# The expert sub-layer's second table: half of its columns by dense products of the whole table, the other half gathered

## The chip, the cores and the metric

The kernel runs on one core of a Trainium2 chip. The metric is device microseconds of one execution, the median of three runs. Engines are named as the profile names them: PE (TensorE matmul), PEld (TensorE weight load), DVE (VectorE), ACT (ScalarE), POOL (GpSimd), SP (SyncE, which here issues DMA alone).

## The reference

One decoder block over 256 tokens of width 2048: a token-mixing sub-layer (two attention mixers that share one input projection), then a channel-mixing sub-layer, PEER. The change is in the second. For each token and each of 8 heads, a product-key search picks 16 of 128 x 128 experts; an expert is one row of `u` and one of `v`, both 16384 x 2048 in float32 (128 MiB each):

```
s1, i1 = lax.top_k(s[:, :, :, 0], PEER_TOPK)          # 16 of 128 first keys
s2, i2 = lax.top_k(s[:, :, :, 1], PEER_TOPK)          # 16 of 128 second keys
expert = i1 * 128 + i2 of the best 16 of 16 x 16 sums;  gate = softmax(top_s)
act = gelu(einsum('cd,ced->ce', hs, u[es]))           # 128 dots of 2048 for each token
y   = einsum('ce,ced->cd', gs * act, v[es])           # weighted sum of 128 rows of v
```

So a token needs 128 rows of `u` and 128 of `v`, 8 KB each. The result is normalised, gated and added to the token.

## The kernel before, in words

Everything is float32. Tokens lie on the 128 partitions, in two tiles (t = 0, 1). Engines run their own instruction streams and meet at semaphores; the order of each stream is written out by hand. The first 700 us (projections, the first tile's attention and mixing) are not touched. From there on:

*First tile's experts beside the second tile's attention and projections.* All engines walk 132 slots `s` (`SLOTS`). In slot `s` DVE takes the dot of the first tile's expert `s` (`dot0`, L2261: multiply a gathered row of `u` by `h2[0]`, both in SBUF, and sum), then a piece of the second tile's attention (slots 5 to 60: `mask_max`, `normalise`, with ACT's exponential between them) or of its projections (`second_projections`, slots 61 to 119: branch outputs, output projection, norms, expert queries), and in some slots a quarter of the next head's top-k (`topk_parts`, L2146). ACT turns four dots into gelu, DVE multiplies by the gates (`coefs`), ACT spreads each coefficient over a diagonal (`diags`, L1003), and PE adds four 512-column products of that diagonal and a gathered row of `v` (`v_row0`, L1644) into four PSUM banks. 192 weight tiles of 512 KB come by SP's queue, the second tile's 96 in a ring of four.

*Gathers.* POOL fetches one row for each of 128 tokens by an indirect DMA (`fetch`, L642, 1 MB): one `u` and one `v` row for each slot, in rings of five; then, for the second tile, in rings of eight, in batches of four (`batch`, L678). An index row is copied to `idx_now` for each head (`take`).

*Second tile's experts.* Eight heads (`unit` on each engine, six of them in a loop): DVE's dots (L2291) and the next head's top-k, ACT's gelu and diagonals, PE's products (L1708) into the other four banks. The first tile's end (`finish(0)`) lies inside the first head, the second's (`finish(1)`) is the kernel's end.

Of the kernel before, what the change touches and what calls it, by code (L numbers as in the profile page):

```python
# [6 lines left out]
ALU = mybir.AluOpType  # L7
# [36 lines left out]
RING0 = 5  # L44
BATCH = 4

# [11 lines left out]
class Chain:  # L58


    def __init__(self, eng, sem):
        self.eng, self.sem, self.n, self.i, self.step = eng, sem, 0, None, 0
# [6 lines left out]
    def wait(self):  # L69
        self.eng.wait_ge(self.sem, self.n if self.i is None else self.i * self.step + self.n)  # L70
# [4 lines left out]

    def enter(self, i, step):
        self.i, self.step, self.n0 = i, step, self.n

    def leave(self, times):
        assert self.n - self.n0 == self.step, (self.n - self.n0, self.step)  # L80
        self.n, self.i = self.n0 + times * self.step, None


def build(nc, x, c, positions, ada_w, ada_b, attn_pre_g, attn_post_g, w_in, cmp_pe, cmp_w1, cmp_b1, cmp_w2,
# [16 lines left out]
    with ExitStack() as ctx:  # L101
# [10 lines left out]
        o_w = o_a + AR * KW  # L112
        o_p = o_w + WR * KW
        o_g = o_p + PR * KW
        o_e = o_g + GR * KW
        o_f = o_e + ER * KW
        o_c = o_f + FR * KW
        o_i = o_c + ACCR * KW
        o_s = o_i + IR * KW
# [88 lines left out]
        gate_f_row = at(o_f + 8 * KW, D)  # L208
# [4 lines left out]
        diag = [at(o_e + 16 * KW + P * i, P) for i in range(8)]  # L213
        sq_junk = at(o_s, NC)
        early_u = [o_f, o_c, o_e, o_e + 8 * KW, o_a]
        early_v = [o_w + 8 * KW, o_w + 16 * KW, o_w + 24 * KW, o_w, o_a + 8 * KW]
        Urow0 = [at(o, D) for o in early_u]
        Vrow0 = [at(o, D) for o in early_v]
        first_free = (PH * TOPK) % RING0
        slots_u = [o_p, o_p + 8 * KW, o_p + 16 * KW] + early_u[first_free:] + early_u[:first_free]  # L220
        slots_v = [o_f + 16 * KW, o_f + 24 * KW, o_i] + early_v[first_free:] + early_v[:first_free]
        Urow = [at(o, D) for o in slots_u]
        slot_sem = [5, 6, 7] + [(first_free + i) % RING0 for i in range(RING0)]
        sem_base = [16 * len(range(i, PH * TOPK, RING0)) if i < RING0 else 0 for i in slot_sem]
        Vrow = [at(o, D) for o in slots_v]
# [31 lines left out]
        mtmp = mod_rows_sb  # L257
# [126 lines left out]
        OUTS = GROUPS + PAIRS  # L384


        LAG = 4
        SLOTS = PH * TOPK + LAG
        FIRST1 = 5
        MIX1 = FIRST1 + 2 * UNITS + 8  # L390
# [142 lines left out]
        def _(pool):  # L533
# [113 lines left out]
            def u_row0(i):  # L647
                u, e = i // TOPK, i % TOPK
                if e == 0:
                    take(u, u % 2)  # L650
# [1695 lines left out]
```

## Time and profile before

| | |
|---|---|
| median of three runs | 2146.29 us (2141.3 to 2150.93) |
| profiled execution: span, first to last instruction | 2140.2 us |
| busy: PE, PEld, DVE, ACT, POOL | 1912.1, 879.8, 1176.6, 389.3, 790.7 us |
| DMA | 821.41 MB, mean 384 GB/s |
| of it, gathers and POOL's other loads (q0) | 637.58 MB, 72.6% of 16 engines' span |
| chain that ended last | PE 51%, DMA 36%, POOL 5%, issue 4%, DVE 3% |

The profile is of one execution. A group of instructions is told by its line in the kernel, its engine and operation, what it writes and reads, and its count; then the time in which at least one of them ran, the mean duration of one, and how long the engine stood idle just before them with what ended the idleness. Busy time of PE overlaps itself, since its matmuls are pipelined. The DMA share is the time that packets took over 16 engines' time, and can come out a little above 1.

### The profile page before, as it was taken

Reading aid. Unit: us, or ns where it says so; the run is one execution under the profiler, and the core shown is the slowest. Engines: PE = TensorE matmul, PEld = TensorE weight load, DVE = VectorE, ACT = ScalarE, POOL = GpSimd, SP = SyncE. Lnnn points to the kernel's source line nnn. Section 1 sums busy time; section 2 is a strip of 40 time slices with the busy share of each in tenths; the row PEclk is TensorE's granted clock in tenths of the full one; section 3 lists DMA queues with packets and bytes.
Section 4 is the critical chain, followed back from the end, with each engine's and each line's share of the span. In section 5 each row is a group of like instructions: output and inputs, shape, how many; then the busy total and the mean of one; then the engine's idle time right before and its main releaser. Section 6 shows DMA issues by size and latency. Waiting matters only on the chain.

```text
span 2140.2 us, 15920 instructions
## 1 busy us (share of the span) xinstructions
PE 1912.1 (89%) x5111; PEld 879.8 (41%) x5111; DVE 1176.6 (55%) x2072; ACT 389.3 (18%) x994; POOL 790.7 (37%) x711
## 2 busy tenths in 40 slices
PE   5999999999999889999999989997778678688687
PEld 3444454444444344554443334442233233233233
DVE  5788657624113567778344445345655655655644
ACT  3111021122211143444010111110201101101101
POOL 4322131100000345666222334456354464454453
PEclk9999999999999999999999999999888889889888
DMA  9999969976897999999999999999999999999997
GB/s 343 367 378 397 374 230 378 373 250 217 284 344 247 386 399 413 417 421 419 417 417 418 417 418 419 417 419 422 422 421 422 422 422 419 422 422 422 422 422 315
DMA packets 161616, 821.41 MB, mean 384 GB/s; under 512 B 17136, under 2 KB 23632, under 8 KB 86796
## 3 DMA queue, kind: packets, MB, share of 16 engines
q0 software_dynamic: 92160, 637.58, 72.6%
q1 hardware_dynamic: 67492, 182.12, 23.5%
q10 hardware_dynamic: 1896, 0.86, 0.2%
q8 instruction: 36, 0.59, 0.1%
q14 instruction: 32, 0.26, 0.0%
HBM read 818.37 MB, written 2.13 MB: 383 GB/s over the span
## 4 chain that ended last, share of the span: by engine, by line
PE 51%; DMA 36%; POOL 5%; issue 4%; DVE 3%; ACT 0%; DVEq 0%; POOLq 0%; SPq 0%; ACTq 0%
PE PS L1153 15%; PE PS L1648 12%; DMA arena<-in_peer_u_dram,idx_now 11%; DMA arena<-in_peer_v_dram,idx_now 11%; PE PS L1609 10%; POOL arena L643 5%; PE PS L1708 5%; DMA arena<-in_peer_w_q_dram 4%; DMA arena<-in_ada_w_dram 4%; DMA arena<-in_w_out_dram 3%; DMA arena<-in_w_branch_mla_dram 2%; PE PS L1215 2%; DVE arena L1779 1%; PE PS L1359 1%; PE PS L1577 1%
## 5 line engine op out<-in xcount | busy, mean ns | idle before, releaser
L1708 PE MATMUL PS<-arena 128*128 128x512 f32 x1008 | 487.1, 647 | 141.0 <-DMA arena<-in_peer_v_dram,idx_now 140.7
L643 POOL DMA_INDIRECT arena<-in_peer_v_dram,idx_now x256 | 356.3, 1392 | 581.9 <-PE PS L1648 323.0
L1648 PE MATMUL PS<-arena 128*128 128x512 f32 x1024 | 471.9, 605 | 20.8 <-DMA arena<-in_peer_v_dram,idx_now 20.8
L2291 DVE CUSTOM_DVE_ANT_0 arena<-arena 128x2048 f32<-128x2048 f32 x128 | 291.9, 2292 | 253.9 <-DMA arena<-in_peer_u_dram,idx_now 253.6
L2264 DVE CUSTOM_DVE_ANT_0 arena<-arena 128x2048 f32<-128x2048 f32 x128 | 292.7, 2290 | 199.0 <-DMA arena<-in_peer_u_dram,idx_now 196.5
L1708 PEld LDWEIGHTS PS<-arena 128*128 128x128 f32 x1008 | 207.6, 209 | 420.4 <-issue 387.6
L643 POOL DMA_INDIRECT arena<-in_peer_u_dram,idx_now x256 | 320.0, 1250 | 147.9 <-issue 70.7
L1609 PE MATMUL PS<-arena 128*128 128x512 f32 x688 | 316.3, 601 | 19.0 <-DMA arena<-in_peer_w_q_dram 9.4
L1153 PE MATMUL PS<-arena 128*128 128x512 f32 x720 | 321.0, 596 | 1.4 <-ACT arena L765 1.4
L1648 PEld LDWEIGHTS PS<-arena 128*128 128x128 f32 x1024 | 191.6, 193 | 253.3 <-issue 220.5
L1609 PEld LDWEIGHTS PS<-arena 128*128 128x128 f32 x688 | 126.3, 190 | 192.4 <-issue 140.8
L1153 PEld LDWEIGHTS PS<-arena 128*128 128x128 f32 x720 | 133.8, 191 | 150.6 <-issue 145.2
L1824 DVE SCALAR_TENSOR_TENSOR arena<-arena,csil 128x2048 f32<-128x2048 f32 x60 | 141.0, 2350 | 19.7 <-DMA arena<-in_ada_w_dram 18.4
L556 POOL DMA_DIRECT2D arena<-in_ada_w_dram x64 | 33.9, 529 | 291.7 <-DVE arena L1824 210.0
L1215 PE MATMUL PS<-arena 128*128 128x512 f32 (+1 forms) x320 | 132.9, 573 | 4.5 <-DVE arena L1759 4.4
L1779 DVE SCALAR_TENSOR_TENSOR arena<-arena,csil 128x512 f32<-128x512 f32 x120 | 90.2, 751 | 20.3 <-DMA arena<-in_ada_w_dram 16.1
L1123 ACT ACTIVATE act_g<-dots 128x4 f32<-128x4 f32 x32 | 6.6, 205 | 500.5 <-DVE dots L2291 500.5
L1005 ACT ACTIVATE arena<-ident,coef 128x128 f32<-128x128 f32 x254 | 81.1, 389 | 82.6 <-DVE coef L2259 82.6
L1215 PEld LDWEIGHTS PS<-arena 128*128 128x128 f32 x320 | 60.6, 193 | 70.7 <-issue 65.0
L544 POOL DMA_DIRECT2D arena<-in_ada_w_dram x64 | 48.0, 754 | 87.5 <-DVE arena L1779 80.7
L638 POOL COPY idx_now<-idx_next 128x16 uint32<-128x16 uint32 x16 | 5.5, 341 | 194.5 <-DVE idx_next L2173 194.4
L1988 DVE CUSTOM_DVE_ANT_0 arena<-PS,causal 128x128 f32<-128x128 f32 (+1 forms) x96 | 30.4, 354 | 66.6 <-PE PS L1359 41.2
(290 smaller groups left out, 1177.0 us busy)
## 6 DMA issues: line engine op xcount, KB each, us to landing
arena<-in_ada_w_dram POOLq DMA_DIRECT2D x64, 1024.0 KB, 8.0
arena<-in_w_in_dram SPq DMA_DIRECT2D x112, 512.0 KB, 8.2
arena<-in_ada_w_dram POOLq DMA_DIRECT2D x64, 512.0 KB, 12.5
arena<-in_w_out_dram SPq DMA_DIRECT2D x64, 512.0 KB, 10.2
arena<-in_peer_w_q_dram SPq DMA_DIRECT2D x64, 512.0 KB, 10.9
arena<-in_w_branch_nsa_dram SPq DMA_DIRECT2D x32, 512.0 KB, 10.0
arena<-in_w_branch_mla_dram SPq DMA_DIRECT2D x32, 512.0 KB, 10.5
arena<-in_x_dram SPq DMA_DIRECT2D x4, 1024.0 KB, 7.8
```

The source lines that it names most:

```text
L544: pool.dma_start(place[:, :, seg, :], ada_v[:, j:j + rows_, c0:c0 + s * P]).then_inc(ada_in[n % ADA_SLOTS], 16)
L643: pool.indirect_dma_start(dst, None, tab, bass.IndirectOffsetOnAxis(ap=idx_now[:, now, e:e + 1], axis=0)).then_inc(landed, 16)
L1005: nc.scalar.activation(diag[e % 8], ident[:, :], ACT.Copy, scale=coef[:, e:e + 1]).then_inc(diag_ready, 1)
L1153: ins = nc.tensor.matmul(PS[:, bank + t, 0:cols], lhs[:, kk, t * P:(t + 1) * P], wring[:, m % WSLOTS, k, 0:cols], start=(kk == 0), stop=(k ...
L1215: ins = nc.tensor.matmul(PS[:, bank + t, 0:cols], hT[:, kk, t * P:(t + 1) * P], wring[:, m % WSLOTS, i, 0:cols], start=(kk == k1), stop=(k ...
L1609: ins = nc.tensor.matmul(PS[:, 4 + a % 2 * 2 + b, :], lhs[:, k, :], tile[:, b * NC:(b + 1) * NC], start=first, stop=last)
L1648: ins = nc.tensor.matmul(PS[:, k, :], diag[i % 8], Vrow0[i % RING0][:, k * NC:(k + 1) * NC], start=(i == 0), stop=False, skip_group_check= ...
L1708: ins = nc.tensor.matmul(PS[:, 4 + k, :], diag[e % 8], Vrow[e % RING][:, k * NC:(k + 1) * NC], start=(first and e == 0), stop=False, skip_ ...
L1779: ins = v.scalar_tensor_tensor(out=part, in0=w, scalar=csil[:, j:j + 1], in1=part, op0=ALU.mult, op1=ALU.add)
L1824: ins = v.scalar_tensor_tensor(out=acc, in0=w, scalar=csil[:, j:j + 1], in1=acc, op0=ALU.mult, op1=ALU.add)
L2264: v.tensor_tensor_reduce(row, row, h2[0], 1.0, 0.0, ALU.mult, ALU.add, dots[:, i % TOPK:i % TOPK + 1]).then_inc(u0_free, 1)
L2291: v.tensor_tensor_reduce(row, row, h2[1], 1.0, 0.0, ALU.mult, ALU.add, dots[:, e:e + 1]).then_inc(u_free, 1)
```

## The change

The 2048 columns of `v` are split at `CD = 1024`.

*Columns 1024 to 2047* are still gathered, as half rows of 512 KB for 128 tokens. The first 64 half rows of the first tile (`V0_ROWS`) are fetched between the second tile's `u` rows and summed on PE with diagonals; the other 192 are fetched behind the last `u` row, in a ring of four (`VRING`), and added on DVE into PSUM (`v_added`).

*Columns 0 to 1023* are computed as a dense product. For each tile a matrix A of 128 x 128 x 128 (first key, second key, token) is built on chip, 64 KB on each partition: the coefficients and both key numbers are turned with PE so that the 128 picks lie on partitions; for each token DVE makes a one-hot of the second key times the coefficient and a one-hot of the first key (`hots`, four tokens at a time, ACT does part of the scaling in `hot_times`), PE multiplies them (`a_rows`), ACT keeps the result (`a_kept`). Then the whole left half of `v` is read in 128 blocks of 128 rows x 1024 columns (512 KB, by SP's queue, a ring of six), and PE multiplies each with both tiles' slices of A. The second tile's A is built while the first 24 blocks (`NB`) go by for the first tile alone; these 24 are read again at the end for the second tile: 152 block reads.

Around it: no row of `v` is fetched in the slots of the first tile (128 slots instead of 132); the rings of `u` rows have eight places throughout; 22 of the first tile's dots and 15 of the second's are multiplied on POOL and summed on ACT (`POOL_ROWS`); from the 17th on, dots read `h2` from PSUM, to which ACT copies it; gelus and coefficients lag by one batch of four; both tiles are finished at the kernel's end; the loops over heads are unrolled; buffers move.

```diff
-RING0 = 5
 BATCH = 4
+CD = 1024
+VRING, DRING = 4, 6
...
+        ROWS = PH * TOPK
+        POOL_ROWS = tuple(range(20, ROWS, 5)) + tuple(range(ROWS + 4, 2 * ROWS - 8, 8))
+        V0_ROWS = ROWS // 2
+        NB = 24
+        BLOCKS = [(j, (0,)) for j in range(NB)] + [(j, (0, 1)) for j in range(NB, NK)] + [(j, (1,)) for j in range(NB)]
...
@@ sync: _(sp) @@
+            sp.wait_ge(u_free, dve_rows(2 * ROWS - 24))
+            sp.wait_ge(u_summed, pool_rows(ROWS))
+            for n, (j, tiles) in enumerate(BLOCKS):
+                if n < 2:
+                    sp.wait_ge(v_free, V0_ROWS)
+                elif n < DRING:
+                    sp.wait_ge(u_free, dve_rows(2 * ROWS))
+                    sp.wait_ge(u_summed, pool_rows(2 * ROWS))
+                else:
+                    sp.wait_ge(d_used, n - DRING + 1)
+                sp.dma_start(Vblk[n % DRING], v_tab[j * P:(j + 1) * P, 0:CD]).then_inc(w_landed[n % DRING], 16)
+                if n == 64:
+                    mod_row(gate_f_row, 3, row_in[0])
...
@@ gpsimd: _(pool) @@
+            def u_product(i):
+                pool.wait_ge(u_in[i % RING], 16 * (i // RING + 1))
+                pool.wait_ge(h2_ready[i // ROWS], 1)
+                row = Urow[i % RING]
+                pool.tensor_tensor(row, row, h2[i // ROWS], ALU.mult).then_inc(u_times, 1)
...
+                if n >= VRING:
+                    pool.wait_ge(v_free, n - VRING + 1)
+                fetch(v_halves, Vrow0[n % VRING], idx_v[0][:, n:n + 1], v_in[n % VRING])
...
+            for i in range(2 * ROWS):
+                u_row(i)
+                if i - RING + 1 in POOL_ROWS:
+                    u_product(i - RING + 1)
+                if i >= ROWS + RING and i % 2 == 0:
+                    v0_row((i - ROWS - RING) // 2)
+            for n in range((ROWS - RING) // 2, V0_ROWS):
+                v0_row(n)
+            for n in range(2 * ROWS - V0_ROWS):
+                v_row(n)
...
@@ scalar: _(act) @@
+            def row_summed(i):
+                act.wait_ge(u_times, pool_rows(i + 1))
+                row, e = Urow[i % RING], i % TOPK
+                nc.scalar.activation(row, row, ACT.Copy, accum_out=dots[:, e:e + 1]).then_inc(u_summed, 1)
...
@@ tensor: _(pe) @@
+            def a_rows(m):
+                t = m // 32
+                pe.wait_ge(hot_scaled, m + 1)
+                if m % 32 >= 2:
+                    pe.wait_ge(a_out, m - 1)
+                for k in range(4):
+                    ins = nc.tensor.matmul(PS[:, 4 * t + m % 2, k * P:(k + 1) * P], hot2[t][m % 2][:, k, :],
+                                           hot1[m % 2][:, k, :], start=True, stop=True)
+                ins.then_inc(a_in, 1)
...
+            def block_products(n):
+                j, tiles = BLOCKS[n]
+                pe.wait_ge(w_landed[n % DRING], block_landed(n))
+                for t in tiles:
+                    for k in range(2):
+                        ins = nc.tensor.matmul(PS[:, 4 * t + k, :], A_T[t][:, j, :], Vblk[n % DRING][:, k * NC:(k + 1) * NC],
...
+            turn_stats(1)
+            pe.wait_ge(a_out, 32)
+            n = 0
+            for m in range(32, 64):
+                a_rows(m)
+                if (m - 31) * NB // 32 > n:
+                    block_products(n)
+                    n += 1
+            pe.wait_ge(a_out, 64)
+            for n in range(NB, len(BLOCKS)):
+                block_products(n)
...
@@ vector: _(dve) @@
+            def hots(m):
+                t, tok = m // 32, 4 * (m % 32)
+                if m >= 2:
+                    dve.wait_ge(a_in, m - 1)
...
+            def v_added(n):
+                t, k = (0, V0_ROWS + n) if n < ROWS - V0_ROWS else (1, n - (ROWS - V0_ROWS))
+                dve.wait_ge(v_in[n % VRING], 16 * ((V0_ROWS + n) // VRING + 1))
+                sums_t = PS[:, 4 * t + 2:4 * t + 4, :].rearrange("p a b -> p (a b)")
+                dve.wait_ge(v_free, V0_ROWS + n)
...
+            for m in range(32, 64):
+                hots(m)
+                if m % 2:
+                    v_added(n)
+                    n += 1
+            for n in range(n, 2 * ROWS - V0_ROWS):
+                v_added(n)
+            finish_first()
+            finish_second()
```

## Rows read from the trace of the kernel before

**Rows 1.** the stretches; columns: us, busy (count) by engine, PE clock, DMA share, GB/s
```profile
...
735.00:1021.00 286.00, 276.65 (x944) 139.24 (x943) 203.12 (x465) 111.72 (x283) 170.60 (x120) 0.98 1.01 414
1021.00:1480.00 459.00, 432.29 (x1029) 184.74 (x1027) 210.65 (x325) 63.26 (x146) 179.71 (x139) 0.99 1.02 418
1480.00:2123.00 643.00, 501.48 (x1035) 213.50 (x1036) 363.14 (x552) 73.59 (x203) 319.00 (x258) 0.87 1.01 422
...
```

**Rows 2.** PE's groups, 1021 to 1480 us: busy us, mean ns, idle before
```profile
...
L1609 PE MATMUL PS<-arena 128*128 128x512 f32 x384 | 183.3, 606 | 12.3 <-DMA arena<-in_w_out_dram 6.1 <-DMA arena<-in_peer_w_q_dram 2.7 <-DMA arena<-in_w_branch_mla_dram 1.9
...
L1525 PE MATMUL PS<-arena,mod_rows_sb 128*128 128x128 f32 x32 | 4.2, 275 | 0.0
...
```

**Rows 3.** DMA queues from 703 us (packets, MB, share); issues (KB, us to landing)
```profile
...
q0 software_dynamic: 73728, 536.90, 89.9%
q1 hardware_dynamic: 15997, 58.15, 10.2%
...
arena<-in_w_out_dram SPq DMA_DIRECT2D x32, 512.0 KB, 12.6
...
```

**Rows 4.** VectorE's groups, 735 to 1021 us
```profile
...
L2264 DVE CUSTOM_DVE_ANT_0 arena<-arena 128x2048 f32<-128x2048 f32 x56 | 128.0, 2288 | 17.7 <-DMA arena<-in_peer_u_dram,idx_now 16.4 <-DVE topi L2143 1.1
L1988 DVE CUSTOM_DVE_ANT_0 arena<-PS,causal 128x256 f32<-128x256 f32 x48 | 18.4, 420 | 1.7 <-PE PS L1359 1.7
...
L1999 DVE RECIPROCAL srec<-ssum 128x2 f32<-128x2 f32 x24 | 3.9, 164 | 35.9 <-ACT arena L850 35.9
...
```

**Rows 5.** one line of POOL: count, ns min/median/max
```profile
...
L710 POOL TENSOR_TENSOR arena<-arena x3: 1259/1274/1702, 2130.6 to 2133.1; 128x512 f32<-128x512 f32 x3
...
```

**Rows 6.** VectorE in order of time, 1663 to 1717 us: start, us
```profile
...
1663.54 0.29 DVE L2136 MAX8 top<-arena 128x8 f32<-128x128 f32 x1
...
1665.86 2.29 DVE L2291 CUSTOM_DVE_ANT_0 arena<-arena 128x2048 f32<-128x2048 f32 x1
...
1668.07 2.28 DVE L2291 CUSTOM_DVE_ANT_0 arena<-arena 128x2048 f32<-128x2048 f32 x1
...
1693.38 0.42 DVE L2155 TENSOR_TENSOR arena<-top 128x256 f32<-128x256 f32 x1
...
1696.87 0.16 DVE L2259 TENSOR_TENSOR coef<-act_g,gate_now 128x4 f32<-128x4 f32 x1
...
1713.26 0.17 DVE L2162 TENSOR_SCALAR ab_u<-topi 128x16 uint32<-128x16 uint32 x1
...
1716.77 0.17 DVE L2259 TENSOR_TENSOR coef<-act_g,gate_now 128x4 f32<-128x4 f32 x1
...
```

**Rows 7.** VectorE's groups by form, whole span
```profile
...
L1824 DVE SCALAR_TENSOR_TENSOR arena<-arena,csil 128x2048 f32<-128x2048 f32 x60 | 141.0, 2350 | 19.7 <-DMA arena<-in_ada_w_dram 18.4
L1779 DVE SCALAR_TENSOR_TENSOR arena<-arena,csil 128x512 f32<-128x512 f32 x120 | 90.2, 751 | 20.3 <-DMA arena<-in_ada_w_dram 16.1 <-DVE arena L1779 0.5
...
L2006 DVE TENSOR_SCALAR arena<-arena,srec 128x128 f32<-128x128 f32 x48 | 12.6, 304 | 0.9
...
L2167 DVE TENSOR_TENSOR arena<-ab_f,iota_f 128x512 f32<-128x512 f32 x16 | 11.1, 692 | 0.6
...
```

**Rows 8.** ScalarE's groups, 735 to 1021 us
```profile
...
L1005 ACT ACTIVATE arena<-ident,coef 128x128 f32<-128x128 f32 x56 | 17.9, 390 | 14.5 <-DVE coef L2259 14.5
...
```

**Rows 9.** POOL and VectorE in order of time, 2110 to 2114 us
```profile
...
2110.05 0.95 POOL L643 DMA_INDIRECT arena<-in_peer_v_dram,idx_now  x1 [0.30 <-issue]
...
2111.16 2.29 DVE L2291 CUSTOM_DVE_ANT_0 arena<-arena 128x2048 f32<-128x2048 f32 x1 [19.64 <-DMA arena<-in_peer_u_dram,idx_now]
...
2112.09 2.19 POOL L643 DMA_INDIRECT arena<-in_peer_v_dram,idx_now  x1 [1.09 <-issue]
...
```

**Rows 10.** U and V gathers (L643), both tables
```profile
...
DMA to landing us min/median/max: 7.2/21.8/36.3
```

**Rows 11.** VectorE's groups by form, 1480 us to the end
```profile
...
L2212 DVE SCALAR_TENSOR_TENSOR PS<-PS,rstd,arena 128x2048 f32<-128x2048 f32 x1 | 2.4, 2360 | 0.0
...
L2214 DVE TENSOR_TENSOR arena<-arena,PS 128x2048 f32<-128x2048 f32 x1 | 2.3, 2286 | 0.0
...
```

More of the change, by code:

```diff
@@ L69, in wait @@
     def wait(self):
[L70 removed]
+        self.eng.wait_ge(self.sem, self.n)
     def link(self, ins):
@@ L690, in _ @@
-            ORDER = ((u_tab, 0), (u_tab, 1), (v_tab, 0), (u_tab, 2), (v_tab, 1), (u_tab, 3), (v_tab, 2), (v_tab, 3))
-            LAST_ORDER = ORDER[:5] + ((v_tab, 2), (u_tab, 3), (v_tab, 3))
-            def unit(r, now, first=False, last=False):
-                take(r + PH, now)
-                if first:
-                    pool.wait_ge(w2_used, MIX)
-                    pool.wait_ge(sc_in, 8)
-                for tab, b in LAST_ORDER if last else ORDER:
-                    batch(r, now, b, tab, first)
@@ L1137, in _ @@
-            unit(0, first=True)
-            with act.Fori(0, PH - 2) as r:
-                unit(r + 1)
-            unit(PH - 1, last=True)
+            for r in range(PH):
+                if r + 1 < PH:
+                    act.wait_ge(idx_ready, r + PH + 1)
+                    fetch(scores[1][:, r + 1, :])
+                for b in range(TOPK // BATCH):
+                    nb = (PH + r) * 4 + b
+                    dots_activated(nb - 1)
+                    if nb == PH * 4:
+                        stat_turned(0)
+                    if nb > PH * 4:
+                        hot_times(nb - PH * 4 - 1)
+                        a_kept(nb - PH * 4 - 1)
+                    for n in range(2):
+                        v0_diag(2 * (nb - PH * 4) + n)
+                    if b == 2 and r + 1 < PH:
+                        gate_exp(r + PH + 1)
+                    for i in range(nb * BATCH, (nb + 1) * BATCH):
+                        if i in POOL_ROWS:
+                            row_summed(i)
@@ L1714, in _ @@
             pe.wait_ge(q_nat, 8)
             pe.wait_ge(sc_out, 8)
-            unit(0, first=True)
-            with pe.Fori(0, PH - 2) as r:
-                unit(r + 1)
-            unit(PH - 1, last=True)
+            turn_stats(0)
+            for m in range(32):
+                if m:
+                    a_rows(m - 1)
+                for n in range(2):
+                    v0_row(2 * m + n)
+            a_rows(31)
+            turn_stats(1)
+            pe.wait_ge(a_out, 32)
+            n = 0
@@ L2299, in unit @@
+            link(v.tensor_copy(iota_k, iota_i[:, :]))
+            for r in range(PH):
+                u = PH + r
+                parts = topk_parts(u + 1) if r + 1 < PH else []
                 for b in range(TOPK // BATCH):
-                    batch(r, b)
+                    nb = 4 * u + b
+                    for i in range(nb * BATCH, (nb + 1) * BATCH):
+                        dot(i)
                     if parts:
                         parts[b]()
-                    coefs(r + PH, b)
```

531 lines of the change are left out of this document (258 added, 273 removed).

## The prediction

> **What bounds the kernel now.** I cut the span at the instructions that begin and end a stage, and read busy time and DMA share of each stretch [rows 1]. To 735 us nothing changes. From 735 to 1021 us (slots 5 to 61, the second tile's attention), from 1021 to 1480 us (slots 61 to 128, its projections) and from 1480 to 2123 us (the second tile's experts) the DMA share is 1.01 to 1.02 at 414 to 422 GB/s, while VectorE is busy for 203 of 286, 211 of 459 and 363 of 643 us. A PE that is "busy" for 277 of 286 us is no second bound: its matmuls overlap, and 384 of 606 ns each are done in 183 us, 0.48 us apiece [rows 2]. So bytes set the time from 735 us on, and the change removes bytes. The question is what each stretch is bound by once they are gone.
>
> **The bytes.** V is now 256 gathers of 1.049 MB, 268.4 MB. After: 256 gathers of half rows, 134.2 MB, and 152 blocks of 0.524 MB, 79.7 MB (24 of the 128 blocks are read twice). V falls by 54.5 MB, which at 418 GB/s is 130 us. But all that is left of V moves as 4 KB packets. From 703 us on, q1, mostly 4 KB packets, moved 58.15 MB in 10.2% of 1438 us, 396 GB/s; q0 with its 8 KB rows 536.9 MB in 89.9%, 415 GB/s [rows 3]. The 213.9 MB that remain cost some 25 us more for that. I price half rows and blocks at 1.32 us each (0.524 MB at 396) and U rows at 2.53 us (1.049 MB at 415). And V no longer runs beside the second tile's attention and projections: it is moved behind them. So I sum by stretch.
>
> **Slots 5 to 61 (286 us now).** 56 U rows need 142 us of DMA, so VectorE and its partners take over. Now: busy 203.1 [rows 1], and 83 us idle, of which 17.7 before dots, nearly all for U's landing, and 35.9 for ScalarE's exponential [rows 4]; 29 are the rest (the gelu, links between its own operations). Nine of the 56 dots go to POOL and ScalarE: 9 x 2.29 = 21 us off, 182 left. The dots now read h2 from PSUM. L1988, the same kind of operation on a PSUM source, takes 0.42 us for 256 columns, against 2.29 for 2048 [rows 4], the same 1.04 ns a column beyond some 0.15 us; so I cost that at nothing (0.1 us for each of 47 would be 5). Of the 29 us I keep 20, since a gelu is asked for a batch later than before; of the 35.9 I keep 12, because ScalarE then waited for transposes that queue behind V's matmuls, and these go. POOL's product of 2048 columns is four times 1.26 us, 5.0 us [rows 5]; VectorE operations with two SBUF sources may have to wait for it: half of 5 us in each of nine, 22. ScalarE's nine row sums stand before the exponentials in its order; they are in the 12. Sum 182 + 20 + 12 + 22 = 236; I take 235. Bounds: 195 (links alone) to 286 (every wait stays).
>
> **Slots 61 to 128 (459 us now).** 67 U rows, 170 us, and 96 weight tiles, 127 us: 297 if DMA never pauses. PE needs 183 us for 384 matmuls [rows 2]. DMA will pause in slots 92 to 99, where the normalisation uses no weights and only four tiles can be fetched ahead, and in the last 12 slots, where ten dots at a pitch of 2.21 us and a top-k of 11.6 [rows 6] pass 30 us of rows slightly. I add 33 for both: 330. The upper bound: if the four weight tiles landed as late as now, 12.6 us after issue [rows 3], 96 x 13 / 4 = 312, with 45 for the normalisation and 37 for the last slots 394. Slot 128 is then reached at 735 + 235 + 330 = 1300 us (now 1480).
>
> **The second tile's U rows (32 batches of four).** VectorE: 113 dots at 2.21 us [rows 6], 250; seven top-k of 2.3 + 2.3 + 3.5 + 3.5 = 11.6 us [rows 6], 81; 32 times the masks of four tokens, 0.69 us for 512 columns and twice some 0.2 (0.30 less the overlap) for 128 [rows 7], 0.42 for 256 (L2155) [rows 6], 1.5 us, 48; coefficients 5. Sum 384. DMA: 120 rows (eight are in the ring already), 303, and 64 half rows, 85: 388. With two bounds this close each stall counts: 15 products on POOL, half of 5 us each, 37. I take 425; bounds 388 and 470. The upper one has two sources: 384 + 15 x 5 = 459; and POOL's order, in which every second U gather is followed by a V half row that waits until PE has freed a slot four half rows back, with all later U gathers behind it. A full row lands in 21.8 us at the median now [rows 10]; the slot is wanted again after two batches, some 25 us. It just fits. The masks' scaling on ScalarE (0.39 us each [rows 8]) and the gathers' issue on POOL (0.95 us and 0.3 of gap [rows 9]) lie beside. The stage ends at 1725 us.
>
> **The blocks and the other 192 half rows.** Nothing of this kind exists now, and all of it comes behind the last U row. SP's queue has only the gate row and the stores behind the blocks.
> First, 6 us to turn the last coefficients and start DMA again. Then the coefficient matrix of the second tile in 32 steps: masks 1.5 us, and in every other step one half row added on VectorE. That add takes 751 ns for 512 columns and 2350 for 2048 [rows 7], so 1.28 for 1024; with the wait on the add before it, 1.45. That is 2.2 us a step, 70 us (57 at the least, with adds that hide; 95 if each mask also waited for ScalarE's 0.78 and PE's matmuls of 0.28 us [rows 2, 8]). DMA moves 50 tiles meanwhile, the filled rings included.
> Then 122 blocks and 172 half rows are left. No row shows how two full queues of 4 KB packets share. I take equal shares: 122 of each at 2 x 1.32 us, 322, and then 50 half rows alone, in a ring of four. A full row lands 7.2 us after issue at the least [rows 10], a half row so in about 5.9; with the add that is 7.4 us for four, 1.86 each, 93. Together 415. Bounds: 294 x 1.32 = 388, and 480 if the blocks went first and 172 half rows then ran at the ring's pace. PE needs 4 x 0.48 = 1.9 us a block, VectorE 1.45 a half row, of 2.64: both hide.
> Last, the end: the final add, 1.5 us; then, as VectorE finishes both tiles behind it, 2.36 and 2.29 us of full-width work for the first [rows 11], two normalisations of about 1 us, gating of 1024 and twice 512 columns, four writes of 0.75 and the store, 15 us against 12 now.
> Sum 6 + 70 + 415 + 1.5 + 15 = 507; I take 505.
>
> Total 1300 + 425 + 505 = 2230 us, against a span of 2140.2. The runs' median, 2146.29, lies 6 us over that span, so I predict 2235. In one sentence: the first two stretches need 439 us of DMA and take 565, so almost all of what the bytes save is idle time there, and the last stretch pays for small packets, a slow start and short rings.
>
> **A rule from the Trainium skill.** The last of POOL's three multiplies took 1.70 us, beside a VectorE multiply with two SBUF sources, the others 1.26 [rows 5]; a gather's issue took 2.19 us beside a dot and 0.95 alone [rows 9]. The Trainium skill, page "SBUF — State Buffer", section "SBUF: two separate sides", says that VectorE and GpSimd share a port by an exclusive lock, held for a whole instruction, which a VectorE operation with two SBUF inputs also takes. By that rule the trace agrees, gathers beside the new dots issue at 0.95 us, and each product on POOL shuts such VectorE operations out in turn: the third rival.
>
> **Rivals.**
> DMA stays full (faster). For it: three stretches with a share of 1.01 and more today [rows 1]. Against it: the attention stretch will have bytes for 142 us and VectorE work for 182. It decides if the waits in that stretch nearly vanish and no ring of four runs dry. Price: 582 MB are moved from 735 to 2123 us now; less 54.5 that is 527 MB, at 415 GB/s 1270 us; with 25 for small packets, 55 that the attention must leave idle and 17 of end, 735 + 1367 = 2102. Chance 0.27.
> Half rows starve beside the blocks (slower still). If a half row then lands as late as a full row now, per byte, 10.9 us [rows 10], a ring of four gives one in 3.1 us: 172 of them 533 us instead of 415, total 2350. For it: the longest waits of today's PE and VectorE are for landing rows; against it: a shorter queue in front of each. It decides if the add's wait for landing stays above 1 us while blocks run. Chance 0.08.
> POOL's products hold VectorE (slower still): 24 products in the two stretches that VectorE bounds, the full 5 us each instead of half, 60 us more, 2290. For it, the stretched multiply [rows 5]; against it, the dots, which are most of VectorE's work, read PSUM. Chance 0.13.
> That leaves 0.52 for the forecast, whose own range is 2170 to 2290.
>
> **Numbers.** About 0.5% is what a measurement can tell from no change. Faster than that are the first rival and the low edges of the forecast's stages: 0.28. Within it 0.09, slower 0.63. Range 2095 to 2310: every stage at its low bound would give about 2080, every one at its high bound far over 2400, but the bounds don't come together.
>
> **What would show it.** The second tile's first dot near 1300 us, with a DMA share well below 1 from 735 to 1000. The last dot near 1725. The last half row some 490 us later, half rows alone at the end. I am wrong if the attention stretch stays below 210 us, the second tile's U rows under 400, or the last stretch under 470; any two of these bring the time to that of before.

## The result and the profile after

The changed kernel took 2441.53 us (median of four runs, 2435.47 to 2446.48) against 2148.61 for the kernel before beside it: a ratio of 1.137, 95% interval 1.134 to 1.140. The direction was forecast, the size was not: 2235 was predicted, with a range to 2310. The profiled execution has a span of 2433.7 us.

The stretches after, cut where the work of each ends (columns as in [rows 1]): attention, projections, the second tile's U rows, the build of the second coefficient matrix, blocks and half rows (to the last half row; the block products run on to 2426).

```profile
...
735.00:981.00 246.00, 149.27 (x496) 93.38 (x495) 210.52 (x447) 110.68 (x243) 108.24 (x72) 0.51 0.68 262
981.00:1330.00 349.00, 214.56 (x481) 88.09 (x479) 184.26 (x292) 67.35 (x103) 125.92 (x81) 0.87 0.88 347
1330.00:1945.00 615.00, 250.64 (x506) 117.37 (x507) 370.57 (x643) 122.82 (x259) 251.10 (x204) 0.64 0.68 267
1945.00:2021.00 76.00, 72.40 (x362) 48.33 (x361) 67.82 (x146) 52.41 (x97) 19.22 (x18) 0.98 0.89 312
2021.00:2410.00 389.00, 385.91 (x899) 169.69 (x898) 227.26 (x179) 6.53 (x16) 161.07 (x172) 1.00 1.01 395
...
```

Where DMA was full from 735 us on [rows 1], it is now at 0.68 and 0.88 in the first two stretches, which the forecast expected, and at 0.68 in the third, which it did not. Only the last is full, at 395 GB/s.

Dots of U rows (here those of rows 61, 128 and 255, the last) mark the stages:

| | slot 61 | slot 128 | last dot | end of the span |
|---|---|---|---|---|
| forecast | 970 | 1300 | 1725 | 2230 |
| measured | 977 | 1330 | 1932 | 2434 |
| error added in the stage | +7 | +23 | +177 | -4 |

Of the first 7 us, 5 lie before the attention: slot 5's dot starts at 740, not 735. One stage carries nearly the whole error: the second tile's U rows took 602 us from first to last dot, not 425. Who waits there, 1400 to 1900 us (the waits; total us, times, longest):

```profile
...
ACT arena L1125 <- PE PS L1733: 393.3, 25, 20.1
...
PE PS L1741 <- DMA arena<-in_peer_v_dram,causal: 293.6, 49, 11.5
POOL arena L659 <- ACT arena L1018: 162.8, 13, 16.7
DVE arena L2331 <- DMA arena<-in_peer_u_dram,arena: 154.0, 66, 9.1
POOL arena L659 <- DVE arena L2233: 87.0, 6, 14.9
...
```

All gathers leave POOL at L659, in one order. It stood 163 us for ScalarE's row sums (L1018) and 87 us for the next head's indices (L2233), 250 of 500 us. VectorE's 154 us for U's landing follow from it: with both stops mended (the run "both" below) VectorE waits for no U row there. The timeline of one such stop (start, us; idle before in brackets):

```profile
...
1512.47 3.78 PE L1741 MATMUL PS<-arena 128*128 128x512 f32 x4 [4.08 <-DMA arena<-in_peer_v_dram,causal]
...
1516.05 1.91 PE L1733 MATMUL PS<-arena 128*128 128x128 f32 x8
...
1518.00 1.02 ACT L1125 COPY arena<-PS 128x512 f32<-128x512 f32 x1 [10.74 <-PE PS L1733]
...
1519.40 1.90 ACT L1018 ACTIVATE arena<-arena 128x2048 f32<-128x2048 f32 x1
...
1521.66 0.97 POOL L659 DMA_INDIRECT arena<-in_peer_u_dram,arena  x1 [16.73 <-ACT arena L1018]
...
1532.28 2.29 DVE L2331 CUSTOM_DVE_ANT_0 arena<-arena,PS 128x2048 f32<-128x2048 f32 x1 [8.96 <-DMA arena<-in_peer_u_dram,arena]
...
1543.51 0.17 DVE L2233 SCALAR_TENSOR_TENSOR arena<-arena 128x16 uint32<-128x16 f32 x1
1543.95 0.94 POOL L659 DMA_INDIRECT arena<-in_peer_u_dram,arena  x1 [14.86 <-DVE arena L2233]
...
```

Read it from the POOL row of 1521.66: the U gather waited 16.73 us for the row sum of 1519.40, by which ScalarE frees the row's slot. That sum stood in ScalarE's order behind the copy of the coefficient matrix (1518.00), which waited for TensorE's `a_rows` (1516.05), which stands on TensorE behind the product of a V half row (1512.47), which waited for its gather: issued by POOL. So it is a ring: POOL's gather, TensorE, ScalarE, and POOL again. The second stop, at 1543.95, lasts 14.86 us: the first row of a head needs indices that VectorE makes (L2233, 1543.51) only in the last batch of the head before, and eight row slots do not cover that.

Single operations came out as priced, but for the block products (L1750), of which more below (the page's groups; busy us, mean ns, idle before):

```profile
...
L2331 DVE CUSTOM_DVE_ANT_0 arena<-arena,PS 128x2048 f32<-128x2048 f32 x203 | 460.0, 2284 | 179.0 <-DMA arena<-in_peer_u_dram,arena 174.4
...
L1750 PE MATMUL PS<-arena 128*128 128x512 f32 x1024 | 445.6, 593 | 3.1 <-DMA arena<-in_peer_v_dram 3.1
...
L2374 DVE SCALAR_TENSOR_TENSOR PS<-arena,mod_rows_sb,PS 128x1024 f32<-128x1024 f32 x127 | 163.7, 1289 | 117.5 <-DMA arena<-in_peer_v_dram,mod_rows_sb 116.8
...
L685 POOL TENSOR_TENSOR arena<-arena 128x2048 f32<-128x2048 f32 x37 | 167.2, 4520 | 0.7
...
L1018 ACT ACTIVATE arena<-arena 128x2048 f32<-128x2048 f32 x37 | 70.5, 1904 | 90.6 <-POOL arena L685 90.6
...
```

Dots with a PSUM operand take 2284 ns [rows 6: 2.29], the half row's add 1289 (forecast 1.28), POOL's product 4520 (5.0).

### The profile page after: what moved, and what is told of

Its sections match the earlier page's. It is cut to its first block and busy times, and to the rows that moved or that the text cites. A ratio compares the mean times of both kernels' runs of the same rounds, so it can differ in the third digit from the quotient of the medians.

```text
span 2433.7 us, 15718 instructions
## 1 busy us (share of the span) xinstructions
PE 1788.6 (73%) x4869; PEld 866.5 (36%) x4869; DVE 1458.1 (60%) x2431; ACT 496.3 (20%) x1069; POOL 775.4 (32%) x729
## 5 line engine op out<-in xcount | busy, mean ns | idle before, releaser
L2331 DVE CUSTOM_DVE_ANT_0 arena<-arena,PS 128x2048 f32<-128x2048 f32 x203 | 460.0, 2284 | 179.0 <-DMA arena<-in_peer_u_dram,arena 174.4
L659 POOL DMA_INDIRECT arena<-in_peer_u_dram,arena x256 | 258.5, 1010 | 902.0 <-DVE arena L2233 380.0
L1741 PE MATMUL PS<-arena 128*128 128x512 f32 x256 | 207.1, 956 | 352.7 <-DMA arena<-in_peer_v_dram,causal 345.8
L1750 PE MATMUL PS<-arena 128*128 128x512 f32 x1024 | 445.6, 593 | 3.1 <-DMA arena<-in_peer_v_dram 3.1
L1642 PE MATMUL PS<-arena 128*128 128x512 f32 x688 | 325.4, 622 | 83.6 <-DMA arena<-in_w_out_dram 31.4
L1186 PE MATMUL PS<-arena 128*128 128x512 f32 x720 | 319.5, 594 | 1.4 <-ACT arena L768 1.4
L1750 PEld LDWEIGHTS PS<-arena 128*128 128x128 f32 x1024 | 192.5, 190 | 239.0 <-issue 229.9
L2374 DVE SCALAR_TENSOR_TENSOR PS<-arena,mod_rows_sb,PS 128x1024 f32<-128x1024 f32 x127 | 163.7, 1289 | 117.5 <-DMA arena<-in_peer_v_dram,mod_rows_sb 116.8
L1741 PEld LDWEIGHTS PS<-arena 128*128 128x128 f32 x256 | 65.1, 280 | 457.4 <-DMA arena<-in_peer_v_dram,causal 398.6
L1642 PEld LDWEIGHTS PS<-arena 128*128 128x128 f32 x688 | 129.3, 196 | 268.4 <-issue 149.2
L1186 PEld LDWEIGHTS PS<-arena 128*128 128x128 f32 x720 | 133.2, 190 | 149.8 <-issue 144.4
L659 POOL DMA_INDIRECT arena<-in_peer_v_dram,causal x128 | 124.8, 975 | 153.6 <-DVE PS L2374 110.0
L659 POOL DMA_INDIRECT arena<-in_peer_v_dram,mod_rows_sb x128 | 119.9, 937 | 162.3 <-DVE PS L2374 160.6
L685 POOL TENSOR_TENSOR arena<-arena 128x2048 f32<-128x2048 f32 x37 | 167.2, 4520 | 0.7
L2374 DVE SCALAR_TENSOR_TENSOR PS<-arena,cstat,PS 128x1024 f32<-128x1024 f32 x64 | 82.4, 1287 | 43.0 <-DMA arena<-in_peer_v_dram,causal 42.6
L1733 PEld LDWEIGHTS PS<-arena 128*128 128x128 f32 x512 | 85.6, 241 | 45.1 <-issue 40.5
L1018 ACT ACTIVATE arena<-arena 128x2048 f32<-128x2048 f32 x37 | 70.5, 1904 | 90.6 <-POOL arena L685 90.6
```

The lines of the kernel that those rows point to most:

```text
L659: pool.indirect_dma_start(dst, None, tab, bass.IndirectOffsetOnAxis(ap=idx, axis=0)).then_inc(landed, 16)
L685: pool.tensor_tensor(row, row, h2[i // ROWS], ALU.mult).then_inc(u_times, 1)
L1186: ins = nc.tensor.matmul(PS[:, bank + t, 0:cols], lhs[:, kk, t * P:(t + 1) * P], wring[:, m % WSLOTS, k, 0:cols], start=(kk == 0), stop=(k ...
L1642: ins = nc.tensor.matmul(PS[:, 4 + a % 2 * 2 + b, :], lhs[:, k, :], tile[:, b * NC:(b + 1) * NC], start=first, stop=last)
L1733: ins = nc.tensor.matmul(PS[:, 4 * t + m % 2, k * P:(k + 1) * P], hot2[t][m % 2][:, k, :], hot1[m % 2][:, k, :], start=True, stop=True)
L1741: ins = nc.tensor.matmul(PS[:, 2 + k, :], diag[n % 4], Vrow0[n % VRING][:, k * NC:(k + 1) * NC], start=(n == 0), stop=(n == V0_ROWS - 1), ...
```

## The experiments

All times stand beside runs of the kernel before on the same chip (2143.6 to 2148.6 us in each). Row 61, 128 and 255 are their dots in the profiled run.

| run | us | ratio to before, 95% | row 61 | row 128 | row 255 |
|---|---|---|---|---|---|
| changed kernel | 2441.5 | 1.134 to 1.140 | 977 | 1330 | 1932 |
| sums first | 2311.5 | 1.074 to 1.079 | 977 | 1334 | 1808 |
| indices early | 2384.1 | 1.108 to 1.114 | 980 | 1336 | 1884 |
| both (sums first, indices early) | 2259.8 | 1.049 to 1.055 | 978 | 1333 | 1759 |
| no products, second tile | 2318.6 | 1.077 to 1.083 | 974 | 1329 | 1815 |
| no products at all, nothing else changed | 2303.5 | 1.072 to 1.076 | 959 | 1308 | 1797 |
| both + seven slots | 2228.4 | 1.036 to 1.041 | 976 | 1300 | 1728 |
| all reorderings + seven slots | 2217.6 | 1.030 to 1.036 | 983 | 1294 | 1722 |
| the same, no second tile's products | 2203.2 | 1.025 to 1.029 | 982 | 1289 | 1697 |
| the same, no products at all | 2175.7 | 1.012 to 1.016 | 959 | 1268 | 1676 |

**Sums first.** ScalarE's order in a batch of the second tile:

```diff
                         hot_times(nb - PH * 4 - 1)
+                    for i in range(nb * BATCH, (nb + 1) * BATCH):
+                        if i in POOL_ROWS:
+                            row_summed(i)
+                    if nb > PH * 4:
                         a_kept(nb - PH * 4 - 1)
...
-                    for i in range(nb * BATCH, (nb + 1) * BATCH):
-                        if i in POOL_ROWS:
-                            row_summed(i)
```

> ScalarE's row sum in the second tile is put ahead of the copy of the coefficient matrix in its batch; nothing else changes. Theory A (the ring GpSimd product -> ScalarE row sum -> GpSimd's next gather is what stretches the second tile's U rows from the forecast 425 us to 615, because the sum stands behind a copy that waits for TensorE): the stage falls to some 470 to 510 us and the time to 2300 to 2340. Theory B (the stage is late because the next head's indices come only in the fourth part of the top-k, and eight row slots can't cover that): no more than 30 us go, 2410 or more. Theory C (TensorE's half clock makes all chains of the stage long, whatever their order): 2400 to 2440.

130 us go, as theory A said; the stage, from row 128's dot to row 255's, falls from 602 to 474. POOL's waits, 1400 to 1800 us:

```profile
...
POOL arena L659 <- DVE arena L2234: 99.5, 6, 17.1
POOL arena L659 <- ACT arena L1018: 41.8, 13, 5.6
...
```

The wait for sums is down from 163 us in 500 to 42 in 400; the wait for indices stays.

**Indices early.** The second tile's top-k for the next head, in its four batches:

```diff
-                return [lambda: halves(0), lambda: halves(1), candidates, experts]
+                if u > PH:
+                    return [lambda: (halves(0), halves(1)), lambda: (candidates(), experts()), lambda: None, gates]
+                return [lambda: halves(0), lambda: halves(1), candidates, lambda: (experts(), gates())]
```

(`experts` ends at the indices; `gates` is its rest.)

> In the second tile the next head's top-k is worked in the first two batches of a head instead of all four, so that its indices are there two batches earlier; the gates stay in the fourth. Theory A: 2390 to 2440, since the ring stays. Theory B: the 6 or 7 stops of up to 14.9 us at a head's first row go (some 100 us), 2330 to 2360. Theory C: 2400 to 2440.

57 us go, more than theory A allowed and less than theory B's 80 to 110: no stop for indices is left, but the first ring takes part of it (1400 to 1850 us):

```profile
...
POOL arena L659 <- ACT arena L1018: 189.3, 12, 17.9
...
```

**Both.**

> Both edits together. Theories A and B together say that the two stops are the whole of the excess: the second tile's U rows come to 425 to 460 us, 2250 to 2290 in all. Theory C: over 2350, with the DMA queues still idle a quarter of the stage and TensorE at half clock in the chains that gate them.

182 us go, 130 + 57 within 5: the two stops are separate, and together the excess. The stage takes 426 us, the forecast's 425. Theory C falls: the clock is at 0.70 here, little above the 0.64 of before the two edits, and the excess is gone all the same. What fills the stage now is VectorE, busy for 414 of 433 us, with DMA at 0.95 (the first row, to be read against 1330 to 1945 above; the second row is the last stretch):

```profile
...
1333.00:1766.00 433.00, 240.91 (x501) 112.73 (x502) 413.96 (x643) 124.34 (x259) 247.31 (x203) 0.70 0.95 378
...
1840.00:2235.00 395.00, 390.94 (x919) 172.41 (x918) 229.27 (x183) 7.93 (x17) 162.01 (x173) 1.00 1.01 393
...
```

**No products in the second tile.** `POOL_ROWS = tuple(range(20, ROWS, 5))`.

> The second tile's 15 GpSimd products and their ScalarE row sums are left to VectorE's fused dots; the first tile's stay. Theory A: the ring is gone altogether and VectorE, busy some 30 us of 50 in that stage, takes 15 more dots of 2.28 us: 2290 to 2340, as with the sums put first. Theory B: 2400 to 2440. Theory C: 2400 to 2440.

As theory A had it: without the sums there is no ring through ScalarE, and POOL's remaining wait is for indices (1400 to 1800 us):

```profile
...
POOL arena L659 <- DVE arena L2233: 166.5, 6, 27.9
...
```

**No products at all, the one part undone.** `POOL_ROWS = ()` in the changed kernel.

> The changed kernel with one part undone: none of its 37 GpSimd products and ScalarE row sums, all 256 rows are VectorE's dots; everything else as changed, the late indices and four weight slots too. If what the products cost is the ring of the second tile plus what they hold of VectorE: 2319 without the second tile's, some 20 less for the attention's (240 to 218 us), 2290 to 2305. If the attention's gain needs the early top-k as well: 2310 to 2325.

138 us go (2303.5, as the first case had it): 18 by row 61, 4 more by row 128, 113 in the second tile's stage.

**The last stretch: what holds it?** Both orders mended, and once the second tile's half rows left out (`for n in range(ROWS - V0_ROWS)` on POOL and VectorE), once half of the block products:

```diff
                     for k in range(2):
+                        if k and j not in (NB * t, NB - 1 if t else NK - 1):
+                            continue
                         ins = nc.tensor.matmul(PS[:, 4 * t + k, :], A_T[t][:, j, :], ...
```

> With both orders mended, and the second tile's 128 half rows of V neither gathered nor added (so those columns of the second tile are not computed). The last stretch, from the last dot of a U row to the end, was 492 us with both orders mended, with TensorE 99% busy and the DMA engines at 1.01. Theory P (TensorE's block products, 1,024 records of 0.43 us, set it): under 15 us go, 2245 or more. Theory Q (the transfers set it, 393 GB/s): 67 MB are 170 us less of transfers, and the time falls by 100 us or more until TensorE holds it, 2100 to 2160. Theory R (the queues make each other slow, so that the block loads of SP's queue pace TensorE): some 50 us, 2210.

> With both orders mended, and of each block's two matmuls per tile only the first is made but at a tile's first and last block (512 columns of V are not computed). Theory P: TensorE's 1,024 records fall to some 520, and the last stretch falls by 60 us or more, to 2200 or less, until the transfers hold it. Theory Q: under 20 us, 2240 or more, since the same 157 MB are moved. If this and the kernel without the second tile's half rows both stay within 20 us of 2260, the two are in balance and either alone is enough to hold it.

2255.96 and 2262.9 us, one run each against 2259.8: neither gives anything, and the last sentence of the second expectation holds. The last stretch without the second tile's half rows, then with half of the block products:

```profile
...
1840.00:2230.00 390.00, 390.00 (x929) 174.16 (x929) 72.60 (x64) 10.65 (x23) 43.29 (x46) 1.00 0.64 228
...
```

```profile
...
1840.00:2230.00 390.00, 245.80 (x463) 81.37 (x461) 210.87 (x164) 2.64 (x8) 152.25 (x163) 0.87 1.00 389
...
```

With 67 MB less, DMA is at 0.64 and TensorE busy for all 390 us; with half the products, TensorE is busy for 246 of 390 and DMA is at 1.00. Two limits of the same height; to gain here, both must fall.

**The first tile's slots.** The forecast gave slots 61 to 128 330 us; they took 353. Three reorderings on the kernel with both orders mended: no products from row 64 on; the top-k in slots 1, 3, 5, 7 of a head; ScalarE's GELU ahead of the slot's other work.

```diff
-        POOL_ROWS = tuple(range(20, ROWS, 5)) + ...
+        POOL_ROWS = tuple(range(20, 64, 5)) + ...
```
```diff
-        TOPK_AT, GEXP_AT = (1, 4, 7, 10), 8
+        TOPK_AT, GEXP_AT = (1, 3, 5, 7), 6
```

> With both orders mended, and the first tile's GpSimd products only for rows 20 to 63, those of the attention; the rows from 64 on, in the stretch of the out projections and queries, are VectorE's dots (VectorE was busy 186 of 353 us there). Theory A carried on (a product on GpSimd and its row sum on ScalarE hold the gathers wherever VectorE has room): the stretch goes from 353 us towards the 290 that its 121 MB take at the 420 GB/s of before: 2200 to 2225. Rival: the stretch is held by TensorE's and ScalarE's projections, as in the kernel before, and nothing goes, 2250 to 2265; or the extra dots delay the merges on VectorE, 2270.

> With both orders mended, the first tile's top-k parts stand in slots 1, 3, 5, 7 of a head instead of 1, 4, 7, 10 (GELU's gate exponent in 6), so that the next head's indices come three slots earlier. In the kernel with both orders mended GpSimd waited for indices 48 us in the attention and 38 us in the mix stage. If these waits hold the two stages as they held the second tile's: some 40 us go, 2220. If the attention is held by VectorE, busy 208 of 240 us, and its chains with TensorE and ScalarE, the wait only changes its name: 2250 to 2265; if the top-k parts then crowd the softmax on VectorE, 2270.

> With both orders mended, ScalarE's GELU of a batch in the first tile's slots stands ahead of the slot's row sums, softmax and projection copies instead of behind them. VectorE waited 75 us for it in the mix stage. If that wait holds the stage: 2225 to 2240. If the stage is held by the projections of the second tile (TensorE waiting for weights, its one 40 us stop at the norm): 2250 to 2265.

> The best that these points give together: both orders mended, no GpSimd products after row 63 of the first tile, the early top-k and the GELU first. If the first tile's waits hold its stages only jointly, as one takes the place of another: 2190 to 2225, still 2% or more above the kernel before, since the last stretch (492 us, TensorE and the transfers both full) is untouched. If not: 2245 to 2265.

2256.2, 2254.3, 2255.7 and, all three together, 2258.2 (ratio 1.050 to 1.055, against 1.049 to 1.055 without them): nothing. With no products there, POOL's stops in the stretch only changed their name, from ScalarE's sums to VectorE's dots (980 to 1333 us):

```profile
...
POOL arena L659 <- DVE dots L2336: 94.7, 28, 25.1
POOL arena L659 <- ACT arena L1018: 81.5, 12, 20.8
...
```
```profile
...
POOL arena L659 <- DVE dots L2336: 228.8, 52, 30.7
...
```

So something else paced the slots. The upper bound of the forecast's term named it: four weight tiles in flight.

```diff
-W2SLOTS = 4
+W2SLOTS = 7
-        wide2 = at(o_p, W2SLOTS, 2 * NC)
+        wide2 = [at(o_p + 4 * KW * i if i < 4 else o_w + 4 * KW * (i - 4), 2 * NC) for i in range(W2SLOTS)]
...
+                if i == 4:
+                    sp.wait_ge(w_used, W_BR + MIX)
```

> With both orders mended, the second tile's weight tiles have seven slots instead of four (three more in room that the first tile's ring leaves free). Theory W (slots 61 to 128 are held by the weights' ring of four, whose tile comes back some 13 us after it was asked for: 96 x 13 / 4 = 312 us and the norm's stop of some 40): the stretch falls from 353 us to 300 to 315, near its 122 MB at 420 GB/s, 290; the time to 2205 to 2225. Rival N (it is held by the second tile's norm chain and the slot order of the engines, whatever the ring): 2250 to 2262.

> As the kernel with all reorderings of the first tile, and seven weight slots. If the weights' ring was what made those reorderings worth nothing: 2190 to 2215, below the kernel with seven slots alone by 5 us or more. If they are worth nothing on their own: the same as that one within 5 us. In either case over the kernel before, whose time needs the last stretch to shrink as well.

31 us go with both orders mended, and the stretch from row 61's dot to row 128's falls from 355 us to 323, DMA from 0.88 to 0.94. TensorE's waits for weight tiles there fall from 84 us to 60. The stretch with four slots, then with seven (columns as in [rows 1]):

```profile
...
980.00:1333.00 353.00, 213.36 (x484) 86.85 (x482) 186.49 (x294) 67.18 (x103) 128.51 (x82) 0.88 0.88 345
...
```
```profile
...
978.00:1300.00 322.00, 207.08 (x484) 86.97 (x482) 191.40 (x295) 68.26 (x106) 129.40 (x82) 0.88 0.94 380
...
```

Theory W holds in kind, though short of its 300 to 315. On the kernel with all reorderings the same three slots give 41, and the stretch 311: the reorderings count once the ring does not hold.

**What the products hold.** The kernels with both orders mended show masks on VectorE (L2360) that last as long as a product beside them (start, us):

```profile
...
1375.34 5.52 DVE L2360 TENSOR_SCALAR arena<-causal,mod_rows_sb 128x128 f32<-128x128 f32 x2
...
1376.25 4.52 POOL L685 TENSOR_TENSOR arena<-arena 128x2048 f32<-128x2048 f32 x1
...
1380.78 0.41 DVE L2362 TENSOR_TENSOR arena<-causal,mod_rows_sb 128x256 f32<-128x256 f32 x1
...
```
```profile
...
L2360 DVE TENSOR_SCALAR arena<-causal,mod_rows_sb x64: 332/338/5266, 1349.0 to 1762.5; 128x128 f32<-128x128 f32 x64
...
```

Two masks that take 0.34 us each at the median last 5.52 together and end with the product of 1376.25, which ends at 1380.77. The Trainium skill, page "SBUF — State Buffer", section "SBUF: two separate sides", has VectorE and GpSimd share a port by an exclusive lock, held for a whole instruction. The trace agrees on the end: the mask ends with the product. The row of the masks begins 0.91 us ahead of the product's, more than the two need, and the trace does not say why the second had not ended by then. A dot whose second operand lies in PSUM is not held: all 203 of the changed kernel take 2.27 to 2.29 us, those beside a product too.

> As the kernel with all reorderings and seven weight slots, without GpSimd's 15 products in the second tile (their rows become VectorE's dots). In that kernel VectorE is busy 414 of 433 us in the second tile's U rows, and eight of its masks, of 0.34 us each otherwise, last until a product beside them ends (5.27 us). Third rival of the forecast (the products hold VectorE): 42 us of held masks and some 3 us for each held coefficient step go, 15 dots of 2.28 us (34 us) come, and the stage stays within 10 us or loses 10 to 20: 2195 to 2220, so that the products gain nothing. If they carry VectorE's load as meant: the stage grows by 25 to 34 us, 2240 to 2252.

> As the one before, and also without GpSimd's nine products in the first tile's attention. VectorE, busy 208 of 238 us there, takes 9 more dots of 2.28 us: by the products' purpose 10 to 20 us more than without the second tile's alone; if they only hold VectorE elsewhere, within 5 us of it.

Without the second tile's products the stage goes from 427 to 407 us, and 14 us go in all. VectorE's busy time falls by 20 us although it makes 15 more dots (34 us), so what the products held there was more, some 54 us by these two rows. The stage with and without them:

```profile
...
1294.00:1722.00 428.00, 237.05 (x485) 110.89 (x486) 411.31 (x638) 121.64 (x251) 243.69 (x200) 0.70 0.95 381
...
```
```profile
...
1289.00:1697.00 408.00, 225.04 (x477) 107.34 (x478) 391.24 (x668) 89.64 (x215) 176.11 (x184) 0.73 0.98 398
...
```

Without the attention's nine, 27 more us go, more than either case expected (1.030 to 1.036, then 1.025 to 1.029, then 1.012 to 1.016, none overlapping). In the attention of the changed kernel they held small steps (mean ns; then the same steps in the kernel without products):

```profile
...
L2052 DVE TENSOR_SCALAR nmax<-smax 128x2 f32<-128x2 f32 x24 | 24.7, 1029 | 0.8
L2065 DVE TENSOR_SCALAR arena<-arena,srec 128x256 f32<-128x256 f32 x48 | 20.2, 463 | 0.9
...
```
```profile
...
L2068 DVE TENSOR_SCALAR arena<-arena,srec 128x256 f32<-128x256 f32 x48 | 14.9, 353 | 0.9
...
L2055 DVE TENSOR_SCALAR nmax<-smax 128x2 f32<-128x2 f32 x24 | 4.1, 170 | 0.8
...
```

The 24 negated maxima (L2052; L2055 in the second kernel), of 0.17 us where nothing holds them, averaged 1.03, and the scalings 463 ns instead of 353: some 26 us, against nine dots of 2.28, 21 us, that the products save. That is 5 of the 27 us. Each product's gather and sum also pass through POOL and ScalarE; what that costs in the attention no run tells apart.

**The removal alone.** The kernel before with half V rows and half their matmuls, and no dense products, so half of V's columns are not computed:

```diff
-    v_tab = peer_v.rearrange("l e d -> (l e) d")
+    v_tab = peer_v.rearrange("l e (h d) -> (l e h) d", h=2)
...
-                for k in range(4):
+                for k in range(2 if i else 4):
```

> The kernel before with only the removal: each V row is gathered as half a row, and only two of its four matmuls are made (the other 1,024 columns of V's product are not computed); nothing is put in their place. Theory S (before is held by its transfers alone, 420 GB/s from 703 us to the end): 134 MB less are 320 us, 1830. Theory T (its stages have other bounds close behind, the attention its chains and TensorE, the mix stage TensorE's projections, the second tile VectorE's dots): 1900 to 2000, so that the gather's removal alone was never worth the whole 320 us, and the dense products would have to cost less than 150 to 250 us to win.

1877.8 us, ratio 0.873 to 0.879: 266 us, between the two theories. Its stretches, cut at the same dots (as in [rows 1]):

```profile
...
735.00:971.00 236.00, 201.66 (x727) 101.50 (x728) 201.85 (x466) 111.61 (x283) 191.84 (x116) 0.92 0.97 376
971.00:1357.00 386.00, 334.42 (x759) 136.43 (x757) 208.55 (x325) 62.66 (x144) 187.66 (x138) 0.95 1.01 403
1357.00:1860.00 503.00, 284.54 (x520) 116.81 (x520) 362.56 (x550) 72.64 (x202) 404.13 (x264) 0.77 1.00 402
...
```

DMA is still full, at 0.97 to 1.01, but with half rows it moves 376 to 403 GB/s and not 414 to 422: that is why 134 MB give 266 us and not the 321 that they are at 418 GB/s. Its attention takes 236 us, and so does the changed kernel's from slot 5's dot (740 to 977), but here V's half rows move beside it, at a share of 0.97 against 0.68. What came in for the other half, and V's place behind the U rows, cost the changed kernel 564 us. 266 of them are taken back by the best version here (2175.7). The 298 that remain: blocks of 79.7 MB at 395 GB/s, 202 us, and idle DMA, 75 us by its shares from 740 to 1753 us (0.2 x 229, 0.02 x 290, 0.03 x 421, 0.15 x 73). That is 277 by a sum, which no run tests; some 20 stay open:

```profile
...
740.00:969.00 229.00, 144.84 (x480) 89.74 (x480) 206.88 (x471) 94.06 (x224) 70.81 (x64) 0.52 0.80 294
969.00:1259.00 290.00, 203.96 (x480) 85.31 (x478) 184.87 (x299) 38.23 (x72) 56.88 (x59) 0.92 0.98 391
1259.00:1680.00 421.00, 229.62 (x489) 109.67 (x490) 403.86 (x683) 94.44 (x224) 182.07 (x189) 0.73 0.97 396
1680.00:1753.00 73.00, 67.90 (x329) 44.53 (x328) 59.66 (x132) 48.05 (x91) 19.17 (x18) 0.98 0.85 298
...
```

None of the runs that compute the whole block beats the kernel before.

## Why the prediction went wrong

*What bounds the kernel before* was right: 134 MB out of its gathers gave 266 us, and DMA stayed full.

*Attention*: 242 us from 735, 236 of them from slot 5's dot; forecast 235, with 22 us for VectorE held by products, of which the two groups above show some 26. The step was right, but it had its own answer in it: 21 us off VectorE for 22 held is nothing won, and I left the products in as harmless.

*Slots 61 to 128*: 353, forecast 330. The upper bound's first two parts (tiles as late as in the kernel before, 312 us by [rows 3], and 45 for the norm: 357) came closest, and the seven slots show that the ring held the stage; how late each tile landed there no view tells. I took the end near the transfers' floor because DMA would be less full; a ring of four still hands out a tile only as often as four landings allow.

*The second tile's U rows, the step that failed*: "I take 425; bounds 388 and 470". Its floors were right (426 with both orders mended). What failed is its list of stalls. I followed POOL's order, where a V half row waits for TensorE ("It just fits"), and took half of 5 us for each product on VectorE. I did not follow ScalarE's order, in which a product's row sum stands behind the matrix's copy and that, by way of TensorE, behind the V half row of the same POOL queue: 130 us. Nor did I ask when a head's indices are there against when POOL wants its first row. In the kernel before V gathers filled POOL's queue meanwhile: from 1480 to 2123 us POOL waited 189 us for V's slots and 2 for indices. Here that cost 57 us, and 182 with the first. "The masks' scaling on ScalarE ... lie beside" was true of durations and said nothing of order.

*The last stretch*: 501 us, forecast 505, right by luck. "PE needs 4 x 0.48 = 1.9 us a block" read records as matmuls: one matmul of 512 columns leaves two records (1,024 in the row of L1750, for 512 matmuls in the code; the 384 of [rows 2] are 96 tiles of two matmuls). A block of both tiles is eight records of 0.43 us, 3.4 us, and TensorE does not hide: it is full beside DMA. Nor were half rows left alone at the end at a ring's pace: the two queues shared DMA at 395 GB/s, the 396 I had priced, the last half row was added at 2408 us, and block products alone went on to 2426. The errors cancel: from 1932 on, the start and the second matrix took 13 and 76 us, not 6 and 70, blocks and half rows 405, not 415, and the end 8, not 16.5.

*Rivals*: DMA did not stay full. Half rows did not starve beside the blocks: the adds of the second tile waited 0.93 us each for landing (117.5 us for 127), under the 1 us that was to decide it. POOL's products did hold VectorE, but that was the smaller part of what they cost: 138 us as one part undone, most of it by the ring that their sums close (130 us by order alone). The price of that rival was 60. As the forecast expected, gathers issue faster beside the new dots: 1.01 us at the mean for U and under 0.98 for V, against 1.25 and 1.39 before.

## What to carry to other kernels

When a change gives an engine a new step, write down what stands ahead of it in that engine's order and what that waits for; if the path comes back to the queue that feeds the step, the time for one round is the least that a step can take, and durations alone do not show it. When a stream of transfers is moved away from a stage, ask which waits it had been covering: here a head's late indices and a ring of four weight tiles. Work given to GpSimd beside VectorE must be priced with what it holds there, and tried without.

## What was not expected of the hardware

A small VectorE step can last as long as a GpSimd instruction beside it: 5.27 us at most for one of 0.34 at the median, eight times among 64, with both orders mended.

TensorE's granted clock is 0.51 in the attention, where it is busy for 149 of 246 us; before it was 0.98 there, busy for 277 of 286 [rows 1]. Inside the second tile's stage it changes from one product to the next. The same four records (two matmuls) took 1.96 us at 1.00, 2.4 GHz, after TensorE had stood idle for 1.39 us, and 3.78 us at 0.50, 1.2 GHz, after it had stood idle for 4.08:

```profile
...
1506.40:1508.40 2.00, 1.96 (x4) 0.68 (x4) 1.85 (x7) 0.86 (x4) 0.00 (x0) 1.00 1.02 426
1512.40:1516.30 3.90, 3.83 (x6) 1.76 (x7) 3.90 (x5) 0.00 (x0) 0.00 (x0) 0.50 0.17 71
...
```

With both orders mended the stage came out at the length of the forecast with the clock at 0.70, VectorE busy for 414 of 433 us; what the clock alone costs there no run shows.

At a DMA share of 1.01 the last stretch moves 395 GB/s in 4 KB packets, the stretches before the change 414 to 422 [rows 1], mostly with 8 KB packets.
